# A decoder layer on one core: the chunk state in three fp32r products, the last block in halves of 256 columns, and sixteen convolutions ended on ACT and GpSimd

## The chip, the cores and the metric

The kernel runs on one core of one Trainium2 chip (trn2). The engines are TensorE (PE; its weight loads are listed as PEld), VectorE (DVE), ScalarE (ACT), GpSimd (POOL) and SyncE (SP), each with an instruction queue of its own that runs in program order and waits on semaphores. The metric is the device time of one execution in microseconds, the median of several runs.

## The reference, cut to what matters

One hybrid layer over 512 tokens of width 1024, in float32: sliding-window attention and a Mamba-2 mixer (SSD) side by side, gated and added, then a gated MLP and a final RMSNorm.

```
xbc = jax.nn.silu(causal_dwconv(xbc, ssd_conv_w[layer], ssd_conv_b[layer]))
...
states = jnp.einsum('bclgn,bclgjp->bcgjpn', bc, xc * decay_states[..., None])
...
h = h + ((jax.nn.silu(gt) * val) @ w_down[layer])
return rmsnorm(h, final_norm_w)
```

(The state of a chunk of 128 tokens is the sum over its tokens of b times the decayed x·dt, 128 x 512 numbers for a group of eight heads.) SiLU of a convolution is computed as (tanh(a) + 1) · a, where a is half the convolution.

## The kernel before, in words

The projections are cut into chunks of 256 columns of weights, listed in `CHUNKS`: after the first ones come four `bc` chunks and then `xs` and `z` chunks in turns, `ga`, `ao`, more `xs` and `z`, `gs`, `so`, `out`, `up` and `down`. A chunk has two units u = 0, 1 (128 columns each). A unit is 24 matmuls of 128 x 128 by 512 columns in fp32r: every float32 operand is split into a rounded part (`w_hi`, `xn_hi`, made by ACT in line 585 for the weights) and the rest (`w_lo`, by DVE in line 870), and `three` (lines 1276 to 1278) multiplies hi·hi, hi·lo and lo·hi. The split of the next chunk's weights stands at the head of each chunk on ACT and DVE, two halves of 1024 columns each.

A unit of `bc` or `xs` ends in a convolution along the tokens. There are 24, numbered k from 0: 0 to 7 are `bc`, 8 to 23 `xs`. On ACT, `conv_acc` (line 786) takes the bias and the first tap out of the PSUM bank; DVE adds three taps (line 1224, 128 x 511, 510 and 509); ACT takes the tanh (line 790); DVE multiplies (line 1229, called the end of the convolution here). There are two banks, one for each u: the matmuls of unit k + 2 write the bank that the taps of convolution k read, so TensorE takes it only when these taps are done. `conv_acc` and `conv_tanh` have two buffers as well, and ACT begins convolution k only when the end of k - 2 is through (semaphore `c_out`).

Attention and SSD work rides between these steps: `RIDES`, a table made from `ATT_STAGES` and `SSD_STAGES`, puts each step of attention step n or SSD chunk n into a slot of a unit, three a unit on ACT and DVE (before the convolution, after its taps, after its end), two on TensorE, one on POOL. Within an attention step, DVE masks the scores and finds the maximum (lines 945 to 953), ACT takes four exponentials (line 623), DVE the denominators (958, 960), POOL divides (line 549, 128 x 512), TensorE transposes and DVE masks again (967, 969). Every second step also has ACT copy a half of the result out of PSUM (`attended`, 630), DVE add the other half (975), ACT round (637) and DVE subtract (983, `a_lo`).

SSD chunk n = 4g + cc (group g, chunk cc): DVE makes x·dt and, decayed, `xdt_decayed` (lines 991, 995), and multiplies the decays (1000); TensorE forms the state product `b_nat_cb` by `xdt_decayed` (line 1387, float32, only for cc below 3), the product with the old state (1392) and eight products (1399).

At the end, `down` chunks 6 to 11 fill four PSUM banks with the right half (512 columns) of each of four token blocks t. For each t, DVE adds the bank to `h` (line 1193), ACT squares and sums (851) and takes the root (853), DVE the reciprocal (1208), and ACT and DVE scale the left (856) and the right half (895) into `final_out`, which the SP queue stores (line 493; the last block in two DMAs).

## Time and profile before

| | us |
|---|---|
| median of 3 runs (lowest, highest) | 1028.66 (1027.56, 1028.87) |
| the profiled execution's own time | 1028.22 |
| its span in the trace | 1026.5 |
| TensorE matmul busy | 1017.6 |
| VectorE busy | 640.3 |
| ScalarE busy | 462.3 |
| GpSimd busy | 88.5 |

The span is the time from the first to the last instruction in the trace; 1.72 us of the execution's own time lie around it. Busy times come from the same profiled execution. Matmuls are pipelined, so their busy time tells that TensorE has work queued; the pace is told by the distance from one start to the next. Times in rows are us from the span's start, a mean of one instruction in ns.

### The profile page before, as it was taken

The numbers are of one execution on the slowest core, as the hardware profiler recorded it, in microseconds if no ns is written. First come the engines' busy times: TensorE is split into PE (matmuls) and PEld (weight loads), VectorE is DVE, ScalarE is ACT, GpSimd is POOL, SyncE is SP. The second block draws the span as 40 slices with busy tenths as digits, with TensorE's granted clock in tenths as the row PEclk, the third lists the DMA queues.
The fourth block names the chain that finished last, engine by engine and source line by source line (L and its number), as shares of the span: only waits on it lengthen the run. The fifth ranks groups of instructions, "written<-read, shape, count | busy, mean of one in ns | idle before, by whom it ended". The sixth has DMA issues, their size and how long they took to land.

```text
span 1026.5 us, 13649 instructions
## 1 busy us (share of the span) xinstructions
PE 1017.6 (99%) x5215; PEld 835.5 (81%) x5215; DVE 640.3 (62%) x901; ACT 462.3 (45%) x826; POOL 88.5 (9%) x128
## 2 busy tenths in 40 slices
PE   9999999999999999999999999999999999999997
PEld 8887777788788888878888888888888888888886
DVE  7646899785475685985854544666666666641332
ACT  6344556555555546665532222544434444331233
POOL 0001001110132120122220100000000000000000
PEclk9999999999999999999999999999999999999999
DMA  7622222225556425445352733123232223232212
GB/s 219 124 85 82 64 80 69 93 68 126 158 147 155 123 72 157 139 112 158 106 192 89 273 131 120 65 82 122 84 122 82 82 89 115 96 129 83 96 69 82
DMA packets 123500, 116.50 MB, mean 113 GB/s; under 512 B 21343, under 2 KB 111783, under 8 KB 123448
## 3 DMA queue, kind: packets, MB, share of 16 engines
q1 hardware_dynamic: 95509, 94.74, 29.7%
q10 hardware_dynamic: 25346, 12.59, 5.2%
q0 software_dynamic: 2592, 8.46, 2.3%
q8 instruction: 35, 0.57, 0.2%
q14 instruction: 18, 0.14, 0.0%
HBM read 109.41 MB, written 6.36 MB: 113 GB/s over the span
## 4 chain that ended last, share of the span: by engine, by line
PE 90%; DVE 7%; ACT 1%; issue 1%; POOL 0%; ACTq 0%; DVEq 0%; POOLq 0%
PE banks L1276 28%; PE banks L1277 27%; PE banks L1278 27%; DVE conv_acc L1224 2%; PE banks L1399 1%; DVE w_lo L870 1%; PE banks L1392 1%; PE banks L1387 1%; PE banks L1351 1%; PE banks L1328 1%; PE banks L1375 1%; PE banks L1338 0%; DVE bc L1229 0%; PE banks L1448 0%; PE banks L1287 0%
## 5 line engine op out<-in xcount | busy, mean ns | idle before, releaser
L870 DVE TENSOR_TENSOR w_lo<-w_raw,w_hi 128x1024 fp32r<-128x1024 f32 (+1 forms) x166 | 200.1, 1246 | 122.3 <-ACT w_hi L585 121.0
L585 ACT ACTIVATE w_hi<-w_raw 128x1024 fp32r<-128x1024 f32 (+1 forms) x166 | 164.1, 1037 | 107.6 <-PE banks L1278 107.6
L1276 PE MATMUL banks<-xn_hi,w_hi 128*128 128x512 f32 x528 | 211.6, 401 | 1.0 <-DVE conv_acc L1224 1.0
L1277 PE MATMUL banks<-xn_lo,w_hi 128*128 128x512 f32 x528 | 206.0, 390 | 0.0
L1278 PE MATMUL banks<-xn_hi,w_lo 128*128 128x512 f32 x528 | 206.0, 390 | 0.0
L1276 PE MATMUL banks<-hn_hi,w_hi 128*128 128x512 f32 (+1 forms) x376 | 141.3, 376 | 0.0
L1277 PE MATMUL banks<-hn_lo,w_hi 128*128 128x512 f32 (+1 forms) x376 | 141.2, 375 | 0.0
L1278 PE MATMUL banks<-hn_hi,w_lo 128*128 128x512 f32 (+1 forms) x376 | 141.2, 375 | 0.0
L1276 PEld LDWEIGHTS banks<-xn_hi,w_hi 128*128 128x128 f32 x528 | 99.2, 188 | 27.0 <-issue 6.0
L1278 PEld LDWEIGHTS banks<-xn_hi,w_lo 128*128 128x128 f32 x528 | 99.1, 188 | 21.5
L1277 PEld LDWEIGHTS banks<-xn_lo,w_hi 128*128 128x128 f32 x528 | 99.3, 188 | 18.9
L1276 PEld LDWEIGHTS banks<-hn_hi,w_hi 128*128 128x128 f32 x376 | 70.8, 188 | 12.8
L1278 PEld LDWEIGHTS banks<-hn_hi,w_lo 128*128 128x128 f32 x376 | 70.8, 188 | 12.8
L1277 PEld LDWEIGHTS banks<-hn_lo,w_hi 128*128 128x128 f32 x376 | 70.8, 188 | 12.6
L1276 PE MATMUL banks<-w_hi,act_hi 128*128 128x512 f32 x176 | 68.5, 389 | 0.0
L1277 PE MATMUL banks<-w_lo,act_hi 128*128 128x512 f32 x176 | 68.5, 389 | 0.0
L1278 PE MATMUL banks<-w_hi,act_lo 128*128 128x512 f32 x176 | 68.5, 389 | 0.0
L1224 DVE SCALAR_TENSOR_TENSOR conv_acc<-banks,half_conv,conv_acc 128x511 f32<-128x511 f32 (+2 forms) x72 | 53.8, 747 | 5.0 <-ACT conv_acc L786 3.2
L1276 PE MATMUL banks<-y_hi,w_hi 128*128 128x512 f32 x128 | 50.0, 391 | 0.0
L1278 PE MATMUL banks<-y_hi,w_lo 128*128 128x512 f32 x128 | 49.8, 389 | 0.0
L1277 PE MATMUL banks<-y_lo,w_hi 128*128 128x512 f32 x128 | 49.8, 389 | 0.0
L1045 DVE SCALAR_TENSOR_TENSOR conv_acc<-banks,param_cols,conv_acc 128x511 f32<-128x511 f32 (+1 forms) x44 | 32.9, 748 | 23.1 <-ACT conv_acc L707 20.3
(223 smaller groups left out, 1457.3 us busy)
## 6 DMA issues: line engine op xcount, KB each, us to landing
w_raw<-in_w_in SPq DMA_DIRECT2D x29, 1024.0 KB, 5.4
w_raw<-in_w_up SPq DMA_DIRECT2D x22, 1024.0 KB, 5.1
decay<-acs_scratch ACTq DMA_DIRECT2D x16, 512.0 KB, 6.2
w_raw<-in_w_ssd_o SPq DMA_DIRECT2D x8, 1024.0 KB, 5.7
w_raw<-in_w_down SPq DMA_DIRECT2D x8, 1024.0 KB, 5.1
w_raw<-in_w_in SPq DMA_DIRECT2D x16, 256.0 KB, 4.6
w_raw<-in_w_attn_o SPq DMA_DIRECT2D x16, 256.0 KB, 4.6
decay_off<-acs_scratch ACTq DMA_DIRECT2D x32, 128.0 KB, 3.7
```

The lines of the kernel that those rows point to most:

```text
L585: A.activation(whi[:, c % 2, lo_:hi_], raw[:, c % 2, lo_:hi_], ACT.Copy).then_inc(w_rounded, 1)
L870: V.tensor_tensor(wlo[:, c % 2, lo_:hi_], raw[:, c % 2, lo_:hi_], f32(whi[:, c % 2, lo_:hi_]), ALU.subtract).then_inc(w_split, 1)
L1045: V.scalar_tensor_tensor(out=acc[:, back:SEQ], in0=PS[:, 2 * j + u, 0:SEQ - back], scalar=FW(2 - back, j, 2 * it + u), in1=acc[:, back:SEQ ...
L1224: V.scalar_tensor_tensor(out=acc[:, back:SEQ], in0=b[:, 0:SEQ - back], scalar=CW(3 - back, t), in1=acc[:, back:SEQ], op0=ALU.mult, op1=ALU ...
L1276: T.matmul(out_, w[0], m[0], start=first, stop=False)
L1277: T.matmul(out_, w[0], m[1], start=False, stop=False)
L1278: return T.matmul(out_, w[1], m[0], start=False, stop=last)
L1328: ins = T.matmul(PS[late * HD:(late + 1) * HD, 2 + 2 * hh + j // 2, c1 - (q0_ + HD - k2_):c1], qT[rows, (g // 2) * GQ + j, q0_:q0_ + HD], ...
L1351: ins = T.matmul(PS[hh * HD:(hh + 1) * HD, (2, 7)[keys], queries * GQ * HD:(queries + 1) * GQ * HD] .rearrange("p (j q) -> p j q", j=GQ), ...
L1375: ins = T.transpose(PS[:, 2, t * P:(t + 1) * P], xs[:, TG * g + t, tok], ident[:, :])
L1387: T.matmul(PS[:, 6, :], bncb[:, 0:P], xcd[:, :], start=True, stop=True)
L1392: T.matmul(PS[:, 4, t * P:(t + 1) * P], st[:, t * P:(t + 1) * P], bc[:, NG + g, tok], start=True, stop=True)
```

## The change

Three parts, and two small edits beside them.

**State product.** For the chunks of groups 0 and 1 (n below 8, cc below 3: six products) ACT rounds b and `xdt_decayed` into `b_nat_hi` and `xdt_decayed_hi`, DVE subtracts, and TensorE calls `three` instead of one float32 matmul. The rest parts are written in place over `b_nat_cb` and `xdt_decayed`. For cc = 3 `xdt_decayed` is no longer made, in all four groups.

**End of convolutions 0 to 15.** ACT adds 1 to the tanh in place, and POOL multiplies it with `conv_acc`; the line-1229 operation of DVE stays for 16 to 23.

**The last block.** For t = 3 of the last `down` chunk, TensorE works through the columns in two halves of 256, into banks 4 and 5; what the earlier chunks summed in bank 3 is added to `h` before. Adding, squaring and weighting follow by quarter; DVE scales 768 columns, ACT 256, and ACT's queue stores its own part.

Beside them, the negated copy of the cumulated decay is dropped (one DVE operation, 128 columns), and `chunk_decay` moves.

```diff
 SSD_STAGES = (
     ("PE", "x_and_bc", 1), ("PE", "products", 4), ("ACT", "load_decay", -7),
     ("ACT", "load_start_decay", 4), ("ACT", "bc_out", 1), ("ACT", "start_decay", 5),
-    ("ACT", "squares", 7), ("ACT", "clamp_0", -3), ("ACT", "clamp_1", -2), ("ACT", "decay", -1), ("DVE", "x_dt", 2),
-    ("DVE", "decayed_cb", 3), ("DVE", "new_state", 5), ("DVE", "gated_y", 5), ("POOL", "mask_cb", 0),
+    ("ACT", "squares", 7), ("ACT", "decayed_hi", 2), ("ACT", "clamp_0", -3), ("ACT", "clamp_1", -2), ("ACT", "decay", -1), ("DVE", "x_dt", 2),
+    ("DVE", "decayed_lo", 3), ("DVE", "decayed_cb", 3), ("DVE", "new_state", 5), ("DVE", "gated_y", 5), ("POOL", "mask_cb", 0),
...
+        b_hi = sb("b_nat_hi", [P, P], 183.5, F32R)
+        b_lo = sb("b_nat_lo", [P, P], 182, F32R)
+        xcd_hi = sb("xdt_decayed_hi", [P, SEQ], 193.5, F32R)
+        xcd_lo_of = [sb(f"xdt_decayed_lo{i}", [P, SEQ], o, F32R) for i, o in enumerate((142, 174))]
...
+                    if kind == "bc" or kind == "xs" and i < 4:
+                        k = 2 * i + u + (8 if kind == "xs" else 0)
+                        dst = bc[:, 2 * i + u, :] if kind == "bc" else xs[:, 2 * i + u, :]
+                        eng.wait_ge(c_one, k + 1)
+                        eng.tensor_tensor(dst, cth[:, u, :], cacc[:, u, :], ALU.mult).then_inc(c_out, 1)
...
+                            eng.wait_ge(d_bl, min((NT - 1) * (n // NT) + min(n % NT, NT - 1), 2 * (NT - 1)))
+                        if n % NT < NT - 1 and n < N_SSD // 2:
+                            A.activation(b_hi[:, :], PS[:, 3, 0:P], ACT.Copy)
                         A.activation(bncb[:, :], PS[:, 3, 0:2 * P], ACT.Copy).then_inc(d_bcs, 1)
+                    elif what == "decayed_hi":
+                        if n % NT < NT - 1 and n < N_SSD // 2:
+                            eng.wait_ge(d_xcd, (NT - 1) * (n // NT) + n % NT + 1)
+                            A.activation(xcd_hi[:, :], xcd_of[n // 8][:, :], ACT.Copy).then_inc(d_xh, 1)
...
+                        if k_conv < 16:
+                            eng.wait_ge(c_tanh, k_conv + 1)
+                            A.activation(cth[:, u, :], cth[:, u, :], ACT.Identity, bias=ones[:, 0:1]).then_inc(c_one, 1)
...
+                if t == NT - 1:
+                    A.activation(fjunk[:, 0:256], h[:, t, 512:768], ACT.Square, accum_out=fss[:, t:t + 1]).then_inc(f_sq, 1)
+                    eng.wait_ge(dn_add, NT + t + 2)
+                    A.activation(fjunk[:, 256:512], h[:, t, 768:D], ACT.Square, accum_out=fpart[:, 0:1]).then_inc(f_sq, 1)
+                    eng.wait_ge(f_sq, NT + t + 2)
+                    eng.wait_ge(f_part, 1)
+                    A.activation(fsd[:, t:t + 1], fpart[:, 0:1], ACT.Sqrt, bias=fpart[:, 1:2], scale=1.0 / D).then_inc(f_sd, 1)
+                    eng.wait_ge(f_rs, t + 1)
+                    eng.wait_ge(f_pre, NT)
+                    A.activation(fo[:, t, 0:256], fo[:, t, 0:256], ACT.Identity, scale=frs[:, t:t + 1]).then_inc(f_left, 1)
+                    eng.wait_ge(f_left, NT)
+                    eng.dma_start(out[0, t * P:(t + 1) * P, 0:256], fo[:, t, 0:256]).then_inc(f_st, 16)
+                    break
...
+                    eng.wait_ge(f_pre, NT + 2)
+                    V.tensor_scalar(fo[:, t, 256:D], fo[:, t, 256:D], frs[:, t:t + 1], None, ALU.mult).then_inc(f_right, 1)
+                    return
...
+            def add_quarter(k, t=NT - 1):
+
+                cols = slice(512 + 256 * k, 768 + 256 * k)
+                V.tensor_tensor(h[:, t, cols], h[:, t, cols], PS[:, 4 + k, 256 * k:256 * k + 256], ALU.add).then_inc(dn_add, 1)
+
+            def weigh_quarter(k, t=NT - 1):
+
+                cols = slice(512 + 256 * k, 768 + 256 * k)
+                V.tensor_tensor(fo[:, t, cols], h[:, t, cols], fnw[:, cols], ALU.mult).then_inc(f_pre, 1)
...
+                        if cc < NT - 1:
+                            V.tensor_tensor(xcd[:, :].rearrange("p (h q) -> p h q", h=HG), xv,
+                                            bcast(ddt[:, cc, hs], HG, HD), ALU.mult).then_inc(d_xcd, 1)
                     elif what == "decayed_cb":
                         eng.wait_ge(d_cbm, n + 1)
                         eng.wait_ge(d_exp, n + 1)
                         V.tensor_tensor(ag, ag, bncb[:, P:2 * P].unsqueeze(1).broadcast_to([P, HG, P]), ALU.mult).then_inc(d_m, 1)
+                    elif what == "decayed_lo":
+                        if cc < NT - 1 and n < N_SSD // 2:
+                            eng.wait_ge(d_bcs, n + 1)
+                            V.tensor_tensor(b_lo[:, :], bncb[:, 0:P], f32(b_hi[:, :]), ALU.subtract).then_inc(d_bl, 1)
+                            eng.wait_ge(d_xh, (NT - 1) * g + cc + 1)
+                            V.tensor_tensor(xcd_lo_of[n // 8][:, :], xcd[:, :], f32(xcd_hi[:, :]),
+                                            ALU.subtract).then_inc(d_xl, 1)
...
+                if kind == "down" and i == 10:
+                    eng.wait_ge(gemm_done, DONE[c, NT - 1])
+                    V.tensor_tensor(h[:, NT - 1, 512:D], h[:, NT - 1, 512:D], PS[:, NT - 1, :], ALU.add).then_inc(f_early, 1)
...
+                            if kind == "down" and nh == 1 and t == NT - 1:
+                                eng.wait_ge(f_early, 1)
+                                add_quarter(0)
+                                final_right(t - 1)
+                                eng.wait_ge(gemm_done, DONE[c, t] + 1)
+                                add_quarter(1)
+                                eng.wait_ge(dn_add, NT + t + 1)
+                                weigh_quarter(0)
+                                eng.wait_ge(f_sq, NT + t + 1)
+                                V.scalar_tensor_tensor(out=fpart[:, 1:2], in0=fss[:, t:t + 1], scalar=1.0 / D, in1=fhb[:, t:t + 1],
+                                                       op0=ALU.mult, op1=ALU.add).then_inc(f_part, 1)
+                                eng.wait_ge(dn_add, NT + t + 2)
+                                weigh_quarter(1)
+                                eng.wait_ge(f_sd, t + 1)
+                                V.reciprocal(frs[:, t:t + 1], fsd[:, t:t + 1]).then_inc(f_rs, 1)
+                                break
...
-                        eng.wait_ge(c_tanh, k_conv + 1)
-                        dst = bc[:, t - 16, :] if kind == "bc" else xs[:, t, :]
-                        V.scalar_tensor_tensor(out=dst, in0=cth[:, u, :], scalar=1.0, in1=acc,
-                                               op0=ALU.add, op1=ALU.mult).then_inc(c_out, 1)
+                        if k_conv >= 16:
+                            eng.wait_ge(c_out, k_conv)
+                            eng.wait_ge(c_tanh, k_conv + 1)
+                            V.scalar_tensor_tensor(out=xs[:, t, :], in0=cth[:, u, :], scalar=1.0, in1=acc,
+                                                   op0=ALU.add, op1=ALU.mult).then_inc(c_out, 1)
...
+                            if n < N_SSD // 2:
+                                eng.wait_ge(d_bl, (NT - 1) * g + cc + 1)
+                                eng.wait_ge(d_xl, (NT - 1) * g + cc + 1)
+                                three(PS[:, 6, :], (b_hi[:, :], b_lo[:, :]),
+                                      (xcd_hi[:, :], xcd_lo_of[0][:, :]), True, True)
+                            else:
+                                T.matmul(PS[:, 6, :], bncb[:, 0:P], xcd[:, :], start=True, stop=True)
...
+                            if kind == "down" and i == 11 and t == NT - 1:
+                                take(4, dn_add, NT)
+                                take(5, dn_add, NT)
+                                for n0 in (0, 256):
+                                    for kt in range(nk):
+                                        cols_ = slice(kt * width + n0, kt * width + n0 + 256)
+                                        ins = three(PS[:, 4 + n0 // 256, n0:n0 + 256], (mh[:, kb + kt, tok], ml[:, kb + kt, tok]),
+                                                    (whi[:, c % 2, cols_], wlo[:, c % 2, cols_]), kt == 0, kt == nk - 1)
+                                    ins.then_inc(gemm_done, 1)
+                                continue
```

What this does to the order of instructions is shown at three places. First, ScalarE between convolution 1 and 3 (`conv_acc` is the start of a convolution, `attended` the copy that VectorE waits for), before:

```order
L790 ACTIVATE conv_tanh<-conv_acc 128x512
L585 ACTIVATE w_hi<-w_raw 128x1024 x2
L623 ACTIVATE probs,small<-scores,small 128x128 x4
L626 ACTIVATE small<-small 128x4
L786 ACTIVATE conv_acc<-banks,half_conv 128x512
L790 ACTIVATE conv_tanh<-conv_acc 128x512
L630 ACTIVATE attended<-banks 128x512
L617 ACTIVATE scores<-banks 128x512
L637 ACTIVATE a_hi<-attended 128x2x4x64
```

The same stretch of ScalarE with the change:

```order
L806 ACTIVATE conv_tanh<-conv_acc 128x512
L809 ACTIVATE conv_tanh<-conv_tanh,ones 128x512
L594 ACTIVATE w_hi<-w_raw 128x1024 x2
L632 ACTIVATE probs,small<-scores,small 128x128 x4
L635 ACTIVATE small<-small 128x4
L802 ACTIVATE conv_acc<-banks,half_conv 128x512
L806 ACTIVATE conv_tanh<-conv_acc 128x512
L809 ACTIVATE conv_tanh<-conv_tanh,ones 128x512
L639 ACTIVATE attended<-banks 128x512
L626 ACTIVATE scores<-banks 128x512
```

One instruction stands behind every tanh; the weights' rounding, the exponentials, the next `conv_acc` and `attended` all stand behind it.

Second, GpSimd from the first attention step to the seventh, where before sixteen `probs` operations stood in a row:

```order
L553 TENSOR_TENSOR probs<-probs,small 128x512 x4
L581 TENSOR_TENSOR bc<-conv_tanh,conv_acc 128x512
L553 TENSOR_TENSOR probs<-probs,small 128x512
L581 TENSOR_TENSOR bc<-conv_tanh,conv_acc 128x512 x2
L553 TENSOR_TENSOR probs<-probs,small 128x512
L581 TENSOR_TENSOR bc<-conv_tanh,conv_acc 128x512 x2
L553 TENSOR_TENSOR probs<-probs,small 128x512
```

The ends of the convolutions moved in between; those of 1, 3 and 5 stand right behind a division of attention.

Third, VectorE at the end of the program, token blocks 2 and 3 (`h<-h,banks` is the sum out of PSUM), before:

```order
L1193 TENSOR_TENSOR h<-h,banks 128x512
L895 SCALAR_TENSOR_TENSOR final_out<-h,small,final_norm_row 128x512
L1208 RECIPROCAL small<-small 128x1
L1193 TENSOR_TENSOR h<-h,banks 128x512
L895 SCALAR_TENSOR_TENSOR final_out<-h,small,final_norm_row 128x512
L1208 RECIPROCAL small<-small 128x1
L895 SCALAR_TENSOR_TENSOR final_out<-h,small,final_norm_row 128x512
```

The same place with the change:

```order
L1265 TENSOR_TENSOR h<-h,banks 128x512
L931 SCALAR_TENSOR_TENSOR final_out<-h,small,final_norm_row 128x512
L1280 RECIPROCAL small<-small 128x1
L937 TENSOR_TENSOR h<-h,banks 128x256
L931 SCALAR_TENSOR_TENSOR final_out<-h,small,final_norm_row 128x512
L937 TENSOR_TENSOR h<-h,banks 128x256
L942 TENSOR_TENSOR final_out<-h,final_norm_row 128x256
L1258 SCALAR_TENSOR_TENSOR small<-small 128x1
L942 TENSOR_TENSOR final_out<-h,final_norm_row 128x256
L1263 RECIPROCAL small<-small 128x1
L929 TENSOR_SCALAR final_out<-final_out,small 128x768
```

The last block's 512-column sum became two of 256 with the scaling of block 2 between them, the weighting by the norm's row moved ahead of the root, and one plain scaling of 768 columns is left behind it.

## Rows read from the trace of the kernel before

**Rows 1.** Busy time of each engine (instructions) in two stretches

```profile
115.00:147.00 32.00, 32.00 (x215) 25.22 (x214) 29.72 (x52) 17.28 (x45) 2.08 (x2) 1.00 0.22 67
147.00:173.00 26.00, 24.99 (x156) 19.26 (x155) 24.18 (x41) 15.47 (x37) 3.48 (x3) 1.00 0.26 81
```

**Rows 2.** Timeline of TensorE at three units: start us, us, idle before

```profile
128.08 0.47 PE L1276 MATMUL banks<-xn_hi,w_hi 128*128 128x512 f32 x1
153.66 0.39 PE L1278 MATMUL banks<-xn_hi,w_lo 128*128 128x512 f32 x1
155.06 0.50 PE L1276 MATMUL banks<-xn_hi,w_hi 128*128 128x512 f32 x1 [1.01 <-DVE conv_acc L1224]
```

**Rows 3.** Line of the state product; the chain, start us, us

```profile
L1387 PE MATMUL banks<-xdt_decayed,b_nat_cb x24: 590/591/697, 262.7 to 500.2; 128*128 128x512 f32 x24
337.31 0.86 PE banks L1387 x2
1020.14 0.23 PE banks L1277
```

**Rows 4.** Timeline of VectorE and TensorE, third chunk of group 0

```profile
287.57 1.70 DVE L1000 TENSOR_TENSOR decay<-decay,b_nat_cb 128x1024 f32<-128x1024 f32 x1
291.19 0.59 PE L1387 MATMUL banks<-xdt_decayed,b_nat_cb 128*128 128x512 f32 x1
```

**Rows 5.** Timeline of ACT between convolutions 1 and 2

```profile
104.98 0.63 ACT L790 ACTIVATE conv_tanh<-conv_acc 128x512 f32<-128x512 f32 x1 [2.38 <-DVE conv_acc L1224]
105.52 1.99 ACT L585 ACTIVATE w_hi<-w_raw 128x1024 fp32r<-128x1024 f32 x2
109.05 0.76 ACT L786 ACTIVATE conv_acc<-banks,half_conv 128x512 f32<-128x512 f32 x1
```

**Rows 6.** Group of ACT whose scale is a column, SBUF to SBUF

```profile
L856 ACT ACTIVATE final_out<-final_out,small 128x512 f32<-128x512 f32 x4 | 2.9, 724 | 0.9 <-DVE small L1208 0.9
```

**Rows 7.** Timeline of VectorE, convolutions 2 to 6

```profile
110.00 2.29 DVE L1224 SCALAR_TENSOR_TENSOR conv_acc<-banks,half_conv,conv_acc 128x511 f32<-128x511 f32 x3
116.65 2.31 DVE L1224 SCALAR_TENSOR_TENSOR conv_acc<-banks,half_conv,conv_acc 128x511 f32<-128x511 f32 x3
122.25 2.83 DVE L870 TENSOR_TENSOR w_lo<-w_raw,w_hi 128x1024 fp32r<-128x1024 f32 x2 [0.50 <-ACT w_hi L585]
125.00 2.30 DVE L1224 SCALAR_TENSOR_TENSOR conv_acc<-banks,half_conv,conv_acc 128x511 f32<-128x511 f32 x3
133.89 1.25 DVE L1229 SCALAR_TENSOR_TENSOR bc<-conv_tanh,conv_acc 128x512 f32<-128x512 f32 x1 [0.41 <-ACT conv_tanh L790]
135.06 2.35 DVE L870 TENSOR_TENSOR w_lo<-w_raw,w_hi 128x1024 fp32r<-128x1024 f32 x2
```

**Rows 8.** Timeline of GpSimd (POOL) over the same stretch

```profile
121.83 1.04 POOL L549 TENSOR_TENSOR probs<-probs,small 128x512 f32<-128x512 f32 x1 [10.62 <-DVE small L960]
133.56 1.04 POOL L549 TENSOR_TENSOR probs<-probs,small 128x512 f32<-128x512 f32 x1 [10.69 <-DVE small L960]
```

**Rows 9.** Timeline of TensorE, products of 256 columns

```profile
659.79 0.28 PE L1278 MATMUL banks<-hn_hi,w_lo 128*128 128x256 f32 x1
659.91 0.28 PE L1276 MATMUL banks<-hn_hi,w_hi 128*128 128x256 f32 x1
```

**Rows 10.** Timelines of VectorE and of SyncE’s queue at the end

```profile
1020.63 0.69 DVE L1193 TENSOR_TENSOR h<-h,banks 128x512 f32<-128x512 f32 x1 [0.75 <-PE banks L1278]
1022.63 0.75 DVE L895 SCALAR_TENSOR_TENSOR final_out<-h,small,final_norm_row 128x512 f32<-128x512 f32 x1
1023.38 0.82 SPq L493 DMA_DIRECT2D out<-final_out  x2
1023.76 0.44 SPq L493 DMA_DIRECT2D out<-final_out  x1
```

**Rows 11.** Groups of VectorE, 128 columns, in two operations

```profile
L1170 DVE TENSOR_TENSOR softplus<-softplus,softplus 128x128 f32<-128x128 f32 x7 | 2.0, 292 | 0.2
L1171 DVE TENSOR_SCALAR softplus<-softplus 128x128 f32<-128x128 f32 x7 | 1.6, 227 | 0.2
```

More of the change, by code:

```diff
@@ L486, in _ @@
             for t in range(NT):
[L487 to L493 removed]
+                if t < NT - 1:
+                    eng.wait_ge(f_left, t + 1)
+                eng.wait_ge(f_right, t + 1)
+                cols = slice(0, D) if t < NT - 1 else slice(256, D)
+                eng.dma_start(out[0, t * P:(t + 1) * P, cols], fo[:, t, cols]).then_inc(f_st, 16)
             eng.wait_ge(f_st, 16 * (NT + 1))
@@ L1302, in rides @@
                         eng.wait_ge(acs_ev, 1)
-                        take(3, acs_nat, 3)
+                        take(3, acs_nat, 2)
                         for t in range(NT):
@@ L1542, in _ @@
                             tok = slice(t * P, (t + 1) * P)
+                            ends = last and not (kind == "down" and t == NT - 1) or kind == "down" and (i, t) in ((5, NT - 1), (10, NT - 1))
+                            if kind == "down" and i == 11 and t == NT - 1:
[8 more added lines that the diff above has]
+                                continue
                             for kt in range(nk):
@@ L1548, in _ @@
                                             (whi[:, ck % 2, cols_], wlo[:, ck % 2, cols_]),
-                                            first and ck == cs[0] and kt == 0, last and ck == c and kt == nk - 1)
+                                            first and ck == cs[0] and kt == 0, ends and ck == c and kt == nk - 1)
                             ins.then_inc(gemm_done, 1)
```

34 lines of the change are left out of this document (13 added, 21 removed).

## The prediction

> **What bounds the kernel now.** I read the busy times by stage first. In the two stretches of the first convolutions TensorE has work in all of 32.00 us and in 24.99 of 26.00, and VectorE is busy for 29.72 and 24.18 of them, ACT for 17.28 and 15.47 [rows 1]. So TensorE is the bound, and VectorE runs almost level with it there. Next the timeline of TensorE: at a normal pace one product follows the other after 0.23 us [rows 3], but between 153.66 and 155.06 there are 1.40 us, 1.17 too many, ended by a tap of VectorE [rows 2]: the matmuls of convolution 10 wait for the taps of 8. That is the one large wait on VectorE in this stage. Nearly as tight is convolution 6: its matmuls start at 128.08 [rows 2], and the taps of 4 end at 125.00 + 2.30 = 127.30 [rows 7], 0.78 us of slack. At the end the last product is followed by a row of VectorE and ACT work from 1020.63 to the last store's issue at 1023.76 [rows 10].
>
> **The state product.** The float32 product takes 0.86 us in the chain, for the two instructions that it is made of (24 instructions in the source line are twelve products); one fp32r product of 512 columns takes 0.23 [rows 3]. Three are 0.69, so six products give 6 x 0.17 = **-1.0 us**. This is pure TensorE time, at a place where it does not wait. The price is work on ACT (two copies, about 0.3 and 0.63 us) and VectorE (two subtractions, about 0.3 and 0.69), in front of the product: 1.9 us if all of it were serial. The cover: for the third chunk VectorE's decays, which stand behind this work now, ended at 287.57 + 1.70 = 289.27, and the product started at 291.19 [rows 4]. That is 1.9 us of slack at a chunk where VectorE was late already; where the copies lie beside other waits the need is smaller. I cost the extra work at nothing; were the cover gone, each product would lose what is over, at most some 0.3 us each, and the lower bound of the part's gain is nothing. The x·dt that is not made any more for cc = 3 (0.6 us of VectorE) and the dropped negation free time that nobody waits for.
>
> **The end of sixteen convolutions: ACT.** VectorE loses an operation of some 0.69 us (0.60 until the next can start). ACT gains one right behind the tanh. Before, the next ACT instruction starts 0.54 us after the tanh starts (104.98 to 105.52), 0.09 before it ends [rows 5]. The addition reads what the tanh wrote, so it must await its end at 0.63; ACT's own operation with a column operand takes 0.72 [rows 6]. So the next instruction starts at about 0.67 + 0.63 = 1.30 instead of 0.54: everything queued on ACT behind a tanh comes **0.75 us later**. Queued there are the rounding of the next weights, the exponentials, `attended`, and the next `conv_acc`; VectorE waits for each. I follow the chain from tap run to tap run, as the distance of the starts, with T the end of the taps before:
> - 1 to 2: before, tanh, two roundings, exponentials and `conv_acc` run back to back and end at 109.05 + 0.76 = 109.81, taps at 110.00 [rows 5, 7]. With 0.75 more they end at 110.56: **+0.6**.
> - 2 to 3 (taps at 116.65 [rows 7]): VectorE's sum `attended` awaits ACT's copy. Before, it followed the tanh (0.70) and the end (0.60), so T + 1.3; now ACT's copy starts at T + 1.33 and takes 0.58, so T + 1.9: **+0.6**.
> - 3 to 4: the subtraction `w_lo` awaits the rounding, which stands behind tanh, addition and exponentials: +0.75. Then comes GpSimd, next paragraph: **+0.7 to +1.7, taken as 1.2**.
> - 4 to 5, 6 to 7: VectorE has its data; it only saves the end: **-0.6** each.
> - 5 to 6, 7 to 8: before, `w_lo` started 1.87 us after the taps' end (135.06 [rows 7] less 133.19, which is 133.89 less 0.70 for the tanh), behind a tanh and an end that GpSimd slowed. Now it awaits addition and first rounding, 1.30 + 1.04 + 0.08 = 2.42: **+0.55** each.
> - 0 to 1: the end of 0 on GpSimd now meets VectorE's `a_lo`: 0 to +0.5, taken as 0.25.
>
> **The end of the convolutions: GpSimd.** In the trace an operation of VectorE that reads two tensors from SBUF stands still while GpSimd works: the end at 133.89 took 1.25 us instead of 0.69, and ended 0.54 after GpSimd's (133.56 + 1.04); the pair of `w_lo` at 122.25 took 2.83 instead of 2.35 and ended 2.2 after GpSimd's at 122.87 [rows 7, 8]. Operations that read PSUM, the taps, keep their 2.30. The new operations (two tensors from SBUF, 512 columns, not in the trace on GpSimd) are like its division: 1.04 us; not less, since that one reads a single tensor, and at most 1.7, if one of VectorE's operations of 0.69 is let in first. Most of them fall beside taps and other PSUM work. The end of 3 doesn't: it stands behind the division, and both fall on `w_lo` (in T: division 3.4 to 4.5, end 4.5 to 5.5, `w_lo` ready at 4.1). If VectorE is kept out throughout, the taps of 4 start at T + 5.5 + 2.25 = 7.75 against 6.04 before, +1.7; if it gets in ahead of the end, +0.7. The trace shows both sides only for one operation, so the middle is taken.
>
> The Trainium skill (SBUF — State Buffer, "SBUF: two separate sides") says that VectorE with two SBUF inputs and GpSimd share a pair of ports under an exclusive lock, held for the whole instruction by whoever starts first. The trace agrees at 133.89 (1.25 us) and at 122.25 (2.83 us); by that rule alone the step 3 to 4 would cost 1.7 us and the sum would be 0.5 higher.
>
> **Sum of this part.** 0.25 + 0.6 + 0.6 + 1.2 - 0.6 + 0.55 - 0.6 + 0.55 = **+2.55** for the taps of 8 (1.8 to 3.3 by the bounds). TensorE's unit of convolution 10 waits for these taps before as well as after, so its start moves by the same 2.55. Part of it shows earlier: the taps of 4 come 2.65 later, 0.78 are slack, so the unit of convolution 6 waits 1.9. Behind convolution 10 the z chunks give VectorE time again; for 12 to 15 the same working gives between 0 and +0.5, taken as 0.15, since 14 gains and 15 loses. Altogether **+2.7**. The ends of the convolutions themselves are in time: nobody needs them before the second next `conv_acc`.
>
> **The last block.** Products of 256 columns follow after 0.12 us (659.79 to 659.91 [rows 9]): 24 x 0.12 = 2.88 against 12 x 0.23 = 2.72 us, +0.16. Then the sum starts at 1020.8 (block 2's scaling is just through), takes about 0.42, square and its sum 0.46, root 0.3, reciprocal 0.16, with gaps of 0.03: the scaling starts at 1022.3 instead of 1022.63 [rows 10]. It has 768 columns. A one-tensor operation of 128 columns takes 227 ns where the two-tensor one takes 292 [rows 11]. If its further columns cost as much as those of the two-tensor operation (292 at 128 columns, 690 at 512: 1.04 ns each), it lasts 0.9 us; if half, 0.56. Taken: half. So the store can be issued at 1022.9; before, its first half was issued at 1023.38 and the second at 1023.76, behind it on the one queue [rows 10]. That is between -0.5 and -0.9; as 512 KB have to go out either way, the earlier one counts, **-0.45** (0 to -0.9).
>
> The Trainium skill (VectorE: DVE Perf Modes, "The perf-mode tier table") gives float32 `tensor_scalar` in SBUF twice the pace of `tensor_tensor`; an estimate from its figure for 2048 columns (1227 ns) is 0.46 us, and the sum would be 0.1 lower. No run here shows the operation yet.
>
> **Sum.** -1.0 + 2.7 - 0.45 = +1.25. On the profiled execution (span 1026.5, its time 1028.22) that is 1029.5; the median of the runs lies 0.44 above it, so the forecast is 1028.66 + 1.25 = **1029.9 us**. Its own range is 1028.7 to 1031.3.
>
> **Rivals.**
> - VectorE's freed time decides (chance 0.20). Eight ends before 153.66 are over 5 us less for an engine that was busy for 29.72 of 32, and ACT had 14 us left [rows 1]. If the addition cost the ACT chain next to nothing, the 1.17 would vanish: 1028.66 - 1.17 - 1.0 - 0.45 = 1026.0. Against it: ACT's chain of rows 5 was back to back already, and it is latency there, not load, that VectorE waits for. It decides if the taps of 8 come over 1.2 us earlier.
> - The two effects cancel (0.15): the lengthening of the chain is made up by the saved ends, the wait of 1.17 stays about as it is, and the other parts give 1028.66 - 1.45 = 1027.2. It takes an addition of half my cost and no block by GpSimd.
> - GpSimd blocks `w_lo` everywhere (0.10). If ACT lags a bit more, the ends of 5, 7, 9 and 11 fall on `w_lo` too, each some 0.85 more: 1029.9 + 3.4 = 1033.3. The place is the head of each chunk; it decides when an end starts more than 2.4 us after the taps.
> - The fp32r products come late (0.03): the gain of 1.0 is lost in waits for `xdt_decayed_lo`; 1030.9.
>
> The forecast keeps 0.52. A measurement of this kernel can tell about 0.2% from no change, 2.06 us: faster is below 1026.6, slower above 1030.7. Faster: most of the first rival, with a little of the second, 0.18. Slower: the upper quarter of the forecast (0.13), the third and most of the fourth, 0.25. The rest, 0.57, is within. The range has to take in most of the first rival and the forecast's upper end: 1026.0 to 1031.5; it leaves out the third rival and the far half of the first.
>
> **What the new trace would show.** Right: the state product as three pieces of 0.23 and none of 0.43 in groups 0 and 1, with no wait ahead; the ACT instruction behind a tanh 1.3 us later instead of 0.54; TensorE idle for 1 to 2 us near 128 and again near 156 for a tap of VectorE; a `w_lo` pair of over 3 us near 124 with GpSimd busy beside it; last products 0.12 apart and one SyncE issue near 2.1 us after them. Wrong: no idle time of TensorE before 160, or the next ACT instruction less than a microsecond after the tanh. What would make the forecast wrong most likely is the chain from tap run to tap run, eight steps that each lean on the one before.

## The result, and the profile after

The changed kernel takes 1032.99 us (median of 6 runs, 1032.31 to 1035.11) against 1028.76 for the kernel before (6 runs, 1027.56 to 1029.39): ratio 1.0045, 95% interval 1.0034 to 1.0056. It is 4.2 us slower. The direction of the forecast (+1.25) was right, the size was not: the time lies outside the range of 1026.0 to 1031.5. The profiled execution took 1032.31 with a span of 1030.5, 4.0 more than before.

First the stretches of the convolutions, as in [rows 1], and three short ones that hold the first wait and what follows it (PEclk is the granted clock of TensorE, 1.00 for 2.4 GHz and 0.50 for 1.2 GHz; a value between them is a mean):

```profile
core 0: us, PE busy (x) PEld busy (x) DVE busy (x) ACT busy (x) POOL busy (x), PEclk, DMA share, GB/s
115.00:147.00 32.00, 29.34 (x169) 22.87 (x168) 26.39 (x40) 19.34 (x42) 8.56 (x7) 0.95 0.22 67
147.00:173.00 26.00, 23.91 (x152) 18.51 (x151) 21.13 (x37) 16.64 (x43) 6.82 (x6) 1.00 0.14 42
126.00:131.00 5.00, 2.38 (x13) 1.77 (x11) 4.93 (x6) 0.90 (x2) 1.68 (x1) 1.00 0.17 34
131.00:133.00 2.00, 1.96 (x6) 1.57 (x7) 1.90 (x4) 1.95 (x3) 0.52 (x1) 0.68 1.08 382
133.00:136.00 3.00, 3.00 (x10) 2.34 (x10) 2.96 (x6) 1.82 (x10) 0.77 (x1) 0.64 0.14 44
```

TensorE, without a gap in the first stretch before, now lacks 2.66 us there, and 2.09 in the second (1.01 before). VectorE is busy for less time than before in both and is still what TensorE waits for. TensorE's timeline names the releaser of the two waits:

```profile
start us, us, engine line op out<-in xcount [idle before <-releaser]
127.78 0.60 PE L1411 MATMUL banks<-ident,probs 128*128 128x128 f32 x4
131.04 0.50 PE L1349 MATMUL banks<-xn_hi,w_hi 128*128 128x512 f32 x1 [2.67 <-DVE conv_acc L1296]
131.38 0.39 PE L1350 MATMUL banks<-xn_lo,w_hi 128*128 128x512 f32 x1
...
158.27 0.39 PE L1351 MATMUL banks<-xn_hi,w_lo 128*128 128x512 f32 x1
160.74 0.50 PE L1349 MATMUL banks<-xn_hi,w_hi 128*128 128x512 f32 x1 [2.09 <-DVE conv_acc L1296]
```

Both are the taps of VectorE that I had named (for the units of convolutions 6 and 10). The unit of convolution 10 starts 5.68 us later than before (160.74 against 155.06 in [rows 2]), and I had said 2.55. What made the taps late stands in VectorE's timeline:

```profile
124.83 1.70 DVE L902 TENSOR_TENSOR w_lo<-w_raw,w_hi 128x1024 fp32r<-128x1024 f32 x1 [0.50 <-ACT w_hi L594]
...
128.69 2.30 DVE L1296 SCALAR_TENSOR_TENSOR conv_acc<-banks,half_conv,conv_acc 128x511 f32<-128x511 f32 x3
130.91 0.74 DVE L990 COPY_PREDICATED scores<-mask_prev,banks 128x512 f32<-128x512 int32 x1
131.68 0.69 DVE L993 TENSOR_REDUCE small<-scores 128x4 f32<-128x512 f32 x1
132.40 0.16 DVE L995 TENSOR_TENSOR small<-small 128x4 f32<-128x4 f32 x1
132.60 1.19 DVE L997 TENSOR_SCALAR small<-small 128x4 f32<-128x4 f32 x1
133.71 0.15 DVE L998 TENSOR_TENSOR small<-small 128x4 f32<-128x4 f32 x1
...
146.39 0.69 DVE L993 TENSOR_REDUCE small<-scores 128x4 f32<-128x512 f32 x1
147.11 0.80 DVE L995 TENSOR_TENSOR small<-small 128x4 f32<-128x4 f32 x1
```

and in GpSimd's beside it:

```profile
124.41 1.04 POOL L553 TENSOR_TENSOR probs<-probs,small 128x512 f32<-128x512 f32 x1 [8.12 <-DVE small L1005]
125.41 2.27 POOL L581 TENSOR_TENSOR bc<-conv_tanh,conv_acc 128x512 f32<-128x512 f32 x1
132.49 1.28 POOL L581 TENSOR_TENSOR bc<-conv_tanh,conv_acc 128x512 f32<-128x512 f32 x1 [4.80 <-ACT conv_tanh L809]
...
146.60 1.30 POOL L581 TENSOR_TENSOR bc<-conv_tanh,conv_acc 128x512 f32<-128x512 f32 x1 [6.54 <-ACT conv_tanh L809]
```

The two engines take turns: division of GpSimd (to 125.45), first half of `w_lo` (to 126.53), end of 3 (to 127.68), second half of `w_lo` (to 128.76). The pair takes 3.93 us against 2.83 before, 1.10 more, and it starts 0.75 later behind ACT: 1.85 together. The prediction had this meeting, as a cost between two bounds. What it had not are the rows at 132.60 and 147.11: an operation on **four columns**, which takes 0.17 us, lasts 1.19 and ends 0.02 after GpSimd does (132.49 + 1.28 = 133.77); the other, 0.16, lasts 0.80 and ends with GpSimd at 147.9. The reduction at 146.39, which also runs beside GpSimd, keeps its 0.69.

The table follows the chain from first tap to first tap, each step as its growth against before, in us (the last six columns are the experiments of the next section). The starts are those of VectorE's rows on `conv_acc`, before 94.10, 102.63, 110.00, 116.65, 125.00, 130.88, 137.93, 144.39, 152.70, and after 94.15, 103.20, 111.17, 118.49, 128.69, 134.98, 142.80, 149.29, 158.38; the experiments below have theirs in the same way.

| step | predicted | after | ACT adds, VectorE multiplies | all ends beside taps | odd ends only | even ends only | addition behind next | GpSimd alone |
|---|---|---|---|---|---|---|---|---|
| 0 to 1 | 0.25 | 0.52 | 0.00 | 0.01 | 0.53 | -0.01 | -0.01 | -0.01 |
| 1 to 2 | 0.6 | 0.59 | 0.75 | 0.60 | 0.58 | 0.60 | -0.16 | -0.16 |
| 2 to 3 | 0.6 | 0.67 | 0.76 | 0.66 | 0.67 | 0.66 | -0.08 | 0.28 |
| 3 to 4 | 1.2 | 1.85 | 0.75 | 0.75 | 0.74 | 1.85 | -0.01 | 1.10 |
| 4 to 5 | -0.6 | 0.41 | -0.02 | -0.62 | 0.43 | -0.61 | -0.60 | 0.97 |
| 5 to 6 | 0.55 | 0.77 | 0.54 | 0.53 | 0.53 | 0.79 | -0.22 | 1.76 |
| 6 to 7 | -0.6 | 0.04 | 0.02 | -0.59 | 0.05 | -0.58 | 0.26 | 0.47 |
| 7 to 8 | 0.55 | 0.78 | 0.53 | 0.52 | 0.53 | 0.79 | -0.02 | 1.71 |
| sum | 2.55 | 5.63 | 3.33 | 1.86 | 4.06 | 3.49 | -0.84 | 6.12 |

The parts that I had as gains are there. ACT's timeline shows the lengthened step, 113.52 to 114.82, 1.30 as predicted:

```profile
113.52 0.63 ACT L806 ACTIVATE conv_tanh<-conv_acc 128x512 f32<-128x512 f32 x1 [2.38 <-DVE conv_acc L1296]
114.19 0.72 ACT L809 ACTIVATE conv_tanh<-conv_tanh,ones 128x512 f32<-128x512 f32 x1
114.82 0.58 ACT L639 ACTIVATE attended<-banks 128x512 f32<-128x512 f32 x1
```

TensorE's timeline shows a state product in three pieces without a wait (compare [rows 3, 4]), and the last rows the scaling and the store's issue (compare [rows 10]):

```profile
296.39 0.39 PE L1351 MATMUL banks<-a_hi,w_lo 128*128 128x512 f32 x1
296.62 0.39 PE L1349 MATMUL banks<-xdt_decayed_hi,b_nat_hi 128*128 128x512 f32 x1
296.85 0.39 PE L1350 MATMUL banks<-xdt_decayed_lo,b_nat_hi 128*128 128x512 f32 x1
297.07 0.39 PE L1351 MATMUL banks<-xdt_decayed_hi,b_nat_lo 128*128 128x512 f32 x1
297.30 0.94 PE L1471 MATMUL banks<-bc,state 128*128 128x128 f32 x7
...
1026.84 0.62 DVE L929 TENSOR_SCALAR final_out<-final_out,small 128x768 f32<-128x768 f32 x1
1027.48 0.33 SPq L497 DMA_DIRECT2D out<-final_out  x1
```

### The profile page after: what moved, and what is told of

It reads as the page before. It is cut to its first block, busy times and chain, and to the rows that moved or that the text cites. A ratio compares the mean times of both kernels' runs of the same rounds, so it can differ in the third digit from the quotient of the medians.

```text
span 1030.5 us, 13760 instructions
## 1 busy us (share of the span) xinstructions
PE 1017.8 (99%) x5233; PEld 838.0 (81%) x5233; DVE 639.4 (62%) x897; ACT 477.6 (46%) x856; POOL 108.0 (10%) x144
## 4 chain that ended last, share of the span: by engine, by line
PE 85%; DVE 9%; ACT 3%; issue 2%; DMA 0%; POOL 0%; SPq 0%; ACTq 0%; DVEq 0%
PE banks L1349 27%; PE banks L1351 26%; PE banks L1350 26%; DVE conv_acc L1296 3%; DVE w_lo L902 2%; PE banks L1478 1%; PE banks L1471 1%; ACT conv_tanh L806 1%; ACT w_hi L594 1%; PE banks L1448 1%; PE banks L1424 1%; DMA w_raw<-in_w_in 0%; DVE scores L990 0%; DVE small L993 0%; ACT probs L632 0%
## 5 line engine op out<-in xcount | busy, mean ns | idle before, releaser
L1350 PE MATMUL banks<-w_lo,act_hi 128*128 128x512 f32 (+1 forms) x180 | 69.2, 384 | 0.0
L1351 PE MATMUL banks<-w_hi,act_lo 128*128 128x512 f32 (+1 forms) x180 | 69.2, 384 | 0.0
L1349 PE MATMUL banks<-w_hi,act_hi 128*128 128x512 f32 (+1 forms) x180 | 69.2, 384 | 0.0
```

Of the source, the lines that this page charges most:

```text
L1349: T.matmul(out_, w[0], m[0], start=first, stop=False)
L1350: T.matmul(out_, w[0], m[1], start=False, stop=False)
L1351: return T.matmul(out_, w[1], m[0], start=False, stop=last)
```

## The experiments

Times are medians; the ratio is to runs of the kernel before on the same chip. The theory after the comparison: GpSimd's new work stops VectorE's small operations as well as `w_lo`, and that is the 3 us I missed; ACT's addition does what I said. Rivals: ACT's addition costs nothing and GpSimd everything; the lower clock behind the wait at 128 (0.68 and 0.64 in the rows above) holds up the chain.

**All ends back on VectorE** (`e1_ends_on_vector`). ACT's addition and GpSimd's loop body are taken out, and VectorE has its line of before:

```
+ V.scalar_tensor_tensor(out=dst, in0=cth[:, u, :], scalar=1.0, in1=acc,
+                        op0=ALU.add, op1=ALU.mult).then_inc(c_out, 1)
```

> The changed kernel with the end of all convolutions back on VectorE and without ACT's addition; the state products and the last block stay changed. Both theories of the loss lie in the part that is undone here, so both expect the other two parts alone: the trace of the changed kernel shows TensorE 1.1 us less late after the six state products (5.66 late before them, 4.52 after), and the end row 0.5 us shorter. 1028.76 - 1.1 - 0.5 = 1027.1 us. If it comes out at 1028.5 or more, the state products or the last block cost something that I did not see.

Measured: 1026.68 against 1028.50, ratio 0.9978 (0.9968 to 0.9988). All steps of the table are 0.00 within 0.01, and the wait at convolution 10 is back (1.37 from product to product, 1.40 before). So the move of the ends alone costs some 6 us (1032.99 less 1026.68 is 6.3, of which the steps hold 5.6), and the other two parts hide part of it in the result.

**The other two parts by themselves.** The first has the kernel before with the state products (and what belongs to them), the second with the last block.

> The kernel before with the state products alone (three fp32r products in groups 0 and 1, the copies and differences for them, no negation, no product for the fourth chunk). Theory A: the gain is TensorE's time alone; from the trace with all ends back on VectorE it is 1.35 us for the six (0.47 late before them, 0.88 early after), so 1028.5 - 1.3 = 1027.2 us, and 1027.5 by my first figure of 1.0. Rival: part of the gain with the ends on VectorE came from the run's start, which lay 0.5 us apart: 1027.9 or more.

> The kernel before with the last block alone (halves of 256 columns, quarter sums and squares, 768 columns scaled in one operation). Theory A: the end comes 0.45 us earlier: 1028.05 us. Rival: the store's own time decides and not its issue, since as many bytes go out: 1028.5 us.

Measured: 1026.82 against 1028.27, ratio 0.9983 (0.9974 to 0.9992), for the state products; 1027.84, ratio 0.9994 (0.9985 to 1.0003), for the last block. In the first trace TensorE gains 1.15 us by the six products, 0.14 to 0.22 each, and 0.2 more up to 387 us whose cause I did not trace. In the second trace the run lies some 0.47 early from its first convolution, and its span is 0.9 shorter, which leaves 0.5 for the end; the times alone don't tell that from nothing. (In the profiled executions the first tap comes between 93.56 and 94.73, which is set almost wholly in the first 12 us of the run; so a difference of two such times holds up to 1 us of that, and the table, which counts from the first tap, doesn't.)

**ACT adds, VectorE multiplies** (`e2_add_on_act_only`): GpSimd has no new work.

```
  ...
+ if k_conv < 16:
+     eng.wait_ge(c_one, k_conv + 1)
+     V.tensor_tensor(dst, cth[:, u, :], acc, ALU.mult).then_inc(c_out, 1)
```

> ACT still adds the one behind each tanh, but VectorE multiplies, so GpSimd has no new work. Theory A (the ACT chain is lengthened, as in my prediction, and the larger part of what was missed comes from GpSimd): every step that ends in ACT's work grows by 0.55 to 0.75 us (1 to 2, 2 to 3, 3 to 4, 5 to 6, 7 to 8, together 3.2), none is saved, since VectorE keeps an operation; the four-column operations last 0.16 us again and the w_lo pairs 2.4 to 2.9. 1027.1 + 3.2 = 1030.3 us. Rival B (GpSimd alone is the cause, ACT's addition is hidden): 1027.1 us, taps of convolution 8 near 152.7.

Measured: 1031.66, ratio 1.0030 (1.0020 to 1.0039). The sum of the steps is 3.33, as expected, so ACT's addition is not hidden, and the first rival falls. It is paid at five of the eight steps and at three not at all. The time is 1.4 higher than expected. TensorE loses 0.9 us at 234.57, where it waits for the taps of 15 (0.96 from product to product, 0.02 in the same place before), and 0.4 at 161.50, where its timeline names VectorE's `probs_t_cur`; the sum of the steps ends ahead of both.

**GpSimd's multiplication beside the next taps** (`e3_end_beside_taps`): ACT and GpSimd do what they do in the changed kernel, but GpSimd starts once VectorE reads PSUM.

```
  eng.wait_ge(c_one, k + 1)
+ if k not in (11, 15):
+     eng.wait_ge(c_tap, 3 * k + 4)
```

> As the changed kernel, but GpSimd's multiplication waits until the first tap of the next convolution is done, so that it works while VectorE reads PSUM (the ends of 11 and 15 excepted). ACT's addition stays where it was. Theory A (3.0 us of the loss are VectorE's operations on SBUF that stand still while GpSimd multiplies: w_lo at 124.83, 126.46, 139.68 and 154.01, and four-column operations at 132.60 and 147.11): these go back to 1.2 and 0.17 us; the steps 3 to 4, 4 to 5, 5 to 6 and 6 to 7 are 0.7, -0.6, 0.55 and -0.6 from those of before, the taps of 8 come 2.2 us later than before instead of 5.7, and the time is 1027.1 + 2.2 = 1029.3 us. Rival C (the clock of TensorE, at 0.64 to 0.68 behind the wait at 128, holds the chain up, GpSimd does not): the wait at 128 is still there in part, and less than 1 us comes back, over 1032.

Measured: 1028.66, ratio 0.9995 (0.9986 to 1.0004). One wait more on GpSimd takes 4.3 us off the changed kernel; 3.8 of it lie in the steps, and in the profiled executions the rest is a first tap that comes 0.59 earlier. The sum of the steps falls from 5.63 to 1.86, and step by step it is my forecast without the locks: 0.60, 0.66, 0.75, -0.62, 0.53, -0.59, 0.52. VectorE's small operation beside GpSimd's former place is short again:

```profile
129.47 0.69 DVE L995 TENSOR_REDUCE small<-scores 128x4 f32<-128x512 f32 x1
130.19 0.16 DVE L997 TENSOR_TENSOR small<-small 128x4 f32<-128x4 f32 x1
130.39 0.17 DVE L999 TENSOR_SCALAR small<-small 128x4 f32<-128x4 f32 x1
```

**The locks in two halves.** The same wait for the odd convolutions alone, whose ends fall on `w_lo`, and for the even ones alone, whose ends fall on the four-column operations.

> As the changed kernel, but only the ends of the odd convolutions (those that fall on w_lo) wait for the first tap of the next one. Theory A, with each step's excess added up one by one: step 3 to 4 goes from +1.85 to +0.75 against before, 5 to 6 from +0.77 to +0.53, 7 to 8 from +0.78 to +0.52, and the steps 4 to 5 (+0.41) and 6 to 7 (+0.04) stay. The taps of 8 come 1.6 us earlier than in the changed kernel: 1033.0 - 1.6 = 1031.4 us. Rival (one lock passes its delay to the next, so that removing a part changes the rest): below 1030.5 or above 1032.5.

> The counterpart: only the ends of the even convolutions (those that fall on VectorE's four-column operations) wait for the first tap of the next one. Theory A: steps 4 to 5 and 6 to 7 go from +0.41 and +0.04 to -0.62 and -0.59, 0 to 1 from +0.52 to about 0, the w_lo pairs keep their length (1697 and 2304 ns near 125). The taps of 8 come 2.2 us earlier than in the changed kernel: 1033.0 - 2.2 = 1030.8 us. Rival (the four-column operations of 1192 and 803 ns are long for another reason): the steps stay, over 1032.

Measured: 1032.05, ratio 1.0031 (1.0019 to 1.0043), for the odd ones; 1030.85, ratio 1.0017 (1.0009 to 1.0026), for the even ones. Each half mends its own steps and leaves the others (table): the odd ones take 1.57 off the chain, the even ones 2.14, together 3.71 of the 3.77 that both take. The odd ones' gain is in `w_lo` (3 to 4, 5 to 6, 7 to 8), 1.60; the even ones' in the four-column operations (4 to 5, 6 to 7), 1.64, and in the subtraction `a_lo` behind convolution 0 (0.53), which I had foreseen. So operations of four columns cost as much as the large `w_lo`. The odd variant is 0.65 slower than I expected; see the clock below. The even one has the expected time (1030.8), but its profiled execution lost 1.5 us to the clock too and had its first tap 0.54 early, so it is the steps that show the effect, and the agreement of the times is partly luck.

**The pairs by themselves** (`e6_port_pairs`). Six operations of VectorE alone, then six with GpSimd multiplying beside them.

> A kernel of its own that leaves out the whole computation (it stores its input): VectorE does six operations of one form alone, then six of the same with three multiplications of 512 columns on GpSimd beside them, for seven forms. Theory (an operation of VectorE that reads SBUF in a way that takes both ports stands still while GpSimd works, however small it is): the two-tensor operation of 512 columns from SBUF takes 0.69 us alone and up to 2 us beside GpSimd; the two-tensor and the one-tensor operation of 4 columns take 0.16 alone and over 0.8 at least once beside it; the operations that read one tensor from PSUM, and the reduction, keep their time. Rival (only long operations, or only two-tensor ones, are shut out): the 4-column operations, or the one-tensor one of them, keep 0.16, and the 1192 ns at 132.60 came from something else.

It was run once. The view of a source line gives minimum, median and maximum in ns of its twelve:

```profile
L54 DVE TENSOR_TENSOR vector_out<-x_in x12: 676/684/1750, 12.6 to 22.6; 128x512 f32<-128x512 f32 x12
L56 DVE TENSOR_TENSOR vector_small<-x_in x12: 149/156/1244, 23.4 to 26.5; 128x4 f32<-128x4 f32 x12
L58 DVE TENSOR_SCALAR vector_small<-x_in x12: 155/164/1254, 27.8 to 30.9; 128x4 f32<-128x4 f32 x12
L60 DVE TENSOR_SCALAR vector_out<-x_in x12: 412/420/1482, 32.3 to 39.3; 128x512 f32<-128x512 f32 x12
L62 DVE SCALAR_TENSOR_TENSOR vector_out<-banks,x_in x12: 743/743/751, 39.9 to 47.3; 128x512 f32<-128x512 f32 x12
L65 DVE TENSOR_TENSOR vector_out<-x_in,banks x12: 677/680/687, 48.1 to 54.8; 128x512 f32<-128x512 f32 x12
L66 DVE TENSOR_REDUCE vector_small<-x_in x12: 675/676/686, 55.7 to 62.4; 128x4 f32<-128x512 f32 x12
```

GpSimd's multiplication takes 1.26 us. Each of the first four forms has three operations near its maximum, one for each of GpSimd's three: VectorE's next operation stands until GpSimd's is through, then goes (with one more behind it where they have four columns), and GpSimd has its turn again. The cost is about the length of GpSimd's operation, whatever VectorE's own: 1.07 of the 1.75 us at 512 columns, 1.09 of the 1.24 at 4. Forms that read a tensor from PSUM, and the reduction, are not touched at all.

The Trainium skill (SBUF — State Buffer, "SBUF: two separate sides") has the rule: VectorE with two SBUF inputs or in a mode that uses both ports, and GpSimd, exclude each other for whole instructions. The runs agree, for four columns as for 1024. I had read the rule and the trace of before for long operations only.

**GpSimd makes the whole end** (`e12_end_on_gpsimd_alone`), tanh * acc and then + acc, without ACT's addition:

> As the changed kernel, but without ACT's addition: GpSimd makes the whole end, a multiplication and then an addition of 512 columns (tanh * acc + acc, which is the same value). ACT's chain is that of before, GpSimd works twice as long. Theory A (VectorE's operations that need the shared ports stand still while GpSimd works, one after the other in turn): step 3 to 4 grows by some 1.3 us against before (w_lo meets division, multiplication and addition), 4 to 5 and 6 to 7 by 0.8 to 1.3 (two of the small operations are stopped), 5 to 6 and 7 to 8 by 2, so 6 to 7 us for the taps of 8: 1027.1 + 6.5 = 1033.6 us (1032 to 1035). Rival B' (what costs is ACT's addition, and GpSimd's work is cheap): 1027 to 1029 us.

Measured: 1036.55, ratio 1.0081 (1.0067 to 1.0095). The steps sum to 6.12, in the 6 to 7 expected, with `w_lo` pairs of up to 4.33 us. Step by step the expectation was less good: 6 to 7 grew by 0.47 instead of 0.8 to 1.3, and the `w_lo` steps by less than was put on them. Above 1033.6, TensorE lost 2.5 us to the clock (next) and waited 1.22 at 245.26 for `probs_t_cur`.

**The wait at 128 filled** (`e9_filled_wait`):

```
+ if k_conv == 7:
+     eng.wait_ge(*freed_by[7])
+     for _ in range(12):
+         T.matmul(PS[:, 7, :], xn_hi[:, 0, 0:P], xn_hi[:, 0, :], start=True, stop=True)
```

> The changed kernel with twelve products more, into a bank that nobody uses then, in TensorE's wait at 128: they take 12 x 0.227 = 2.7 us of the 2.94. They only fill the wait, the output doesn't depend on them. Theory A: the clock stays at 1.0 and the unit of convolution 6 takes 5.7 instead of 7.35 us, but nobody waited for that unit: the taps of 8 start near 158.4 as before, TensorE waits some 1.6 us longer ahead of convolution 10, and the time stays at 1033.0 us. Rival C (the lower clock is part of the 4.2 us): 1031.4 us or less.

Measured: 1033.83 (1031.62 to 1034.48), ratio 1.0045 (1.0032 to 1.0059). The windows of its trace:

```profile
131.00:136.00 5.00, 5.00 (x23) 3.89 (x22) 4.90 (x9) 3.62 (x12) 1.29 (x1) 1.00 0.55 189
160.00:162.00 2.00, 0.65 (x3) 0.56 (x4) 1.96 (x4) 0.64 (x2) 0.00 (x0) 1.00 0.84 295
162.00:164.00 2.00, 2.00 (x7) 1.52 (x6) 0.49 (x1) 2.00 (x8) 0.00 (x0) 0.52 0.00 0
164.00:166.00 2.00, 2.00 (x10) 1.36 (x12) 1.26 (x4) 1.49 (x5) 1.09 (x2) 0.63 0.00 0
```

The clock stays at 1.00 (2.4 GHz) from 131 to 136, as expected, and the first tap of 8 comes no earlier, 64.26 us after that of 0 (64.23 in the changed kernel). So the lower clock behind the first wait costs nothing, and that rival falls: in the changed kernel TensorE loses 1.6 us to it (2.97 late against before at 131.04, 4.57 at 135.25), and the next wait takes them up. But TensorE now waits 3.01 us from product to product at 161.35, and there the clock does fall. Nothing is waited for behind it, so it is lost: from the first tap of 8 to that of 12 it takes 53.41 us instead of 51.80, 1.6 more. One of the six runs had a mean clock of 1.00 and took 1031.62, the others 0.998 and 1033.4 to 1034.5. (1031.62 is 0.7 under the fastest execution of the changed kernel; the spread of the first tap covers that, and it is the steps that decide here: they sum to 5.66, as against 5.63.) The even variant shows the same behind its second wait:

```profile
160.00:162.00 2.00, 2.00 (x6) 1.36 (x5) 0.59 (x3) 2.00 (x9) 0.40 (x1) 0.50 0.00 0
```

0.50 is the lower level, 1.2 GHz, and products follow every 0.43 us instead of 0.23. The odd variant lost 1.6 in that place too, and the one with GpSimd alone 2.5 (its unit of 10 starts 5.64 late, and what follows is 8.09 late by 166). In the profiled execution of the changed kernel the clock was at 1.00 behind the second wait; in its slower executions (1033.95 and 1035.11) it may not have been, of which there is no trace.

**ACT's addition behind the next `conv_acc`** (`e4_add_behind_next`), the version that follows from these:

```
  rides(c, u, 1)
+ if 0 < k_conv < 16 and k_conv != 12:
+     eng.wait_ge(c_tanh, k_conv)
+     A.activation(cth[:, 1 - u, :], cth[:, 1 - u, :], ACT.Identity, bias=ones[:, 0:1]).then_inc(c_one, 1)
  eng.wait_ge(c_tap, 3 * k_conv + 3)
  ...
```

(The addition behind the tanh stays for 11 and 15 alone.)

> As the changed kernel, but ACT's addition for convolution k stands behind the conv_acc of k+1 and what rides there, when ACT waits for the taps anyway (own place kept for 11 and 15). GpSimd's multiplication then falls beside the taps of k+1. Theory A: neither the ACT chain nor GpSimd costs anything, and VectorE saves 0.6 us in the steps that it decides (4 to 5, 6 to 7) and 0.2 in others, so the taps of 8 come over 1.2 us earlier than before and the wait of 1.17 us near 155 is gone: 1027.1 - 1.2 = 1025.9 us. Rival B (GpSimd alone): the same, since its work lies beside taps. Rival D (the ends come too late for the second next conv_acc): some conv_acc waits for GpSimd, 1028 or more.

Measured: 1025.72 (1025.11 to 1026.27), ratio 0.9969 (0.9957 to 0.9981): faster than both kernels, 7.3 us under the changed one, with the same operations on the same engines. Its windows, and ACT's row for the moved addition:

```profile
115.00:147.00 32.00, 32.00 (x214) 25.14 (x213) 27.33 (x47) 21.31 (x52) 9.60 (x8) 1.00 0.22 67
147.00:173.00 26.00, 25.81 (x161) 20.02 (x160) 23.41 (x39) 18.32 (x41) 8.57 (x7) 1.00 0.27 81
```

```profile
123.44 0.72 ACT L807 ACTIVATE conv_tanh<-conv_tanh,ones 128x512 f32<-128x512 f32 x1
126.57 0.63 ACT L810 ACTIVATE conv_tanh<-conv_acc 128x512 f32<-128x512 f32 x1 [2.42 <-DVE conv_acc L1300]
```

ACT makes it in time in which it would wait for the taps (2.42 us are left even so), GpSimd's multiplication starts with the taps, and TensorE's wait at convolution 10 is down to 0.19. Against all ends on VectorE this is 1.0 us better by the times and 0.8 by the steps, towards the 1.17 of the first rival.

The steps gave 0.84 and not the "over 1.2" expected. Step 6 to 7 was expected to gain 0.6 and lost 0.26: there VectorE's `a_lo` follows the taps and still meets GpSimd:

```profile
138.57 1.53 DVE L1032 TENSOR_TENSOR a_lo<-attended,a_hi 128x512 fp32r<-128x512 f32 x1
...
138.26 1.29 POOL L581 TENSOR_TENSOR bc<-conv_tanh,conv_acc 128x512 f32<-128x512 f32 x1 [4.81 <-ACT conv_tanh L807]
```

It takes 1.53 us instead of 0.68, 0.85 more, which is the difference. The time came out as expected (1025.9) all the same, in the profiled execution by a first tap that came 0.52 earlier than before.

## Why the prediction was wrong

- **The state product: right in kind, a little small.** -1.0 was forecast, and TensorE gains 1.15 from the six. No wait appeared.
- **The end on ACT: right.** The next instruction comes after 1.30 us as forecast, and with GpSimd kept aside the steps are those of the prediction within 0.1.
- **The end on GpSimd: this step failed.** "Most of them fall beside taps and other PSUM work" left out the three operations of four columns between them. Steps 4 to 5 and 6 to 7, put at -0.6 each because VectorE "only saves the end", were +0.41 and +0.04: 1.01 and 0.64 of the missing 3.08. With the even ends beside the taps they are -0.61 and -0.58. A size was off too: the multiplication was taken at 1.04 us like the division, and takes 1.26 to 1.30.
- **Step 3 to 4: mis-sized.** Taken at 1.2 between bounds of 0.7 and 1.7, it was 1.85. The lower bound rested on `w_lo` getting in ahead of the end. It did (from 125.45 to 126.53), but only its first half; the second half then waited for the end, so the pair met division and end in full. The middle between the bounds had no ground. By the rule of the Trainium skill (SBUF — State Buffer, "SBUF: two separate sides") the prediction had 1.7 there, which was nearer. Steps 0 to 1, 5 to 6 and 7 to 8 were 0.22 to 0.27 above the forecast each, from the same cause: the ends that began at 138.78 and 153.10 were still running when `w_lo` began (139.68 and 154.01), and the forecast put that at nothing. These four make 0.65 + 0.27 + 0.22 + 0.23 = 1.37.
- **TensorE's waits: right place, longer.** 2.67 us idle at 131.04 and 2.09 at 160.74 instead of 1 to 2. Convolutions 12 to 15 cost 0.16 (0.15 forecast).
- **The last block: right.** The scaling of 768 columns took 0.62 us (0.56 taken; the other estimate, 0.46, was further off), the store's issue is at 1027.48, and the trace leaves -0.5 (-0.45 forecast), which the times alone can't show.
- **The sum.** 0.05 + 5.63 + 0.16 for the convolutions, -1.15 and some -0.17 for the state products and behind them, -0.5 for the end: +4.0, the difference of the spans. The medians differ by 4.2. The remaining 0.06 of the missing 3.08 lie in the steps 1 to 2 and 2 to 3.
- **The rival "GpSimd blocks `w_lo` everywhere"** (1033.3) came close to the time by a mechanism that is only partly the real one: `w_lo` was held up at three places, and as much was lost in operations of four columns.

## What to carry to other kernels

- When work goes to GpSimd, list every VectorE operation that can run beside it, with its operands, and the small ones first: a two-tensor operation or a `tensor_scalar` that reads SBUF alone costs up to GpSimd's whole operation, whatever its width (a reduction cost nothing; other forms, such as the reciprocal, were not tried). Put GpSimd's work beside VectorE's reads of PSUM; here one wait for that was worth 3.8 us in the steps, 4.3 in the time.
- An operation added right behind its producer on an engine that others wait for is paid wherever they do (here in five steps of eight, 0.5 to 0.8 us each); the same operation put where that engine waits anyway was free. Moving the additions by one place turned +4.2 us into some -3, of which 1.8 are the other two parts of the change.
